# Latent attention: the five filler matmuls of a step in one group behind the transposes, instead of two in front and three behind

## What is computed

```python
q = (rmsnorm_2(c_q_raw, q_norm) @ w_uq)      # 8 heads x (64 + 32)
kv = (rmsnorm_2(c_kv_raw, kv_norm) @ w_ukv)  # 8 heads x (64 + 64)
s = (qn @ k_nope + qr @ k_rope) * scale      # per head and block of 128 queries
s = where(causal, s, -inf)
p = softmax(s)
o = p @ v
...
merged = sigmoid(gate_mla) * y_mla + sigmoid(gate_gdn) * y_gdn
```

## Time and profile before

| | |
|---|---|
| device time, three runs | 2192.75, 2192.87 and 2186.02 us (median 2192.75) |
| the profiled execution's own time | 2192.44 us |
| its span in the profile | 2190.4 us (2.0 us lie around it) |
| busy: TensorE matmul, VectorE, ScalarE, GpSimd | 94%, 38%, 34%, 36% of the span |
| the chain that ended last | 86% TensorE, 5% VectorE, 3% issue, 2% ScalarE, 2% GpSimd |
| mean granted clock of TensorE | 0.971 of full speed |
| the attention loop | from 1306.3 to 1425.2 us |

### The profile page before, as it was taken

One profiled execution on the slowest core, in us unless ns is written; L12 is line 12 of the kernel. 1 busy time (PEld: TensorE's weight loads), 2 busy tenths in 40 slices (PEclk: granted clock), 3 DMA queues, 4 the chain that ended last, 5 costly groups with the idle time before them and its releaser, 6 DMA issues.

```text
span 2190.4 us, 31427 instructions
## 1 busy us (share of the span) xinstructions
PE 2058.2 (94%) x13672; PEld 1765.2 (81%) x13672; DVE 831.7 (38%) x1270; ACT 737.1 (34%) x1089; POOL 781.8 (36%) x248
## 2 busy tenths in 40 slices
PE   7999999979988879999999989998998899999998
PEld 5898888858866669999999867797777678888886
DVE  3400675144357645220222141275466554211222
ACT  5332223236555534221223243332212333222222
POOL 4433223435422144434433421034313254434432
PEclk9999999989999989999999989998999999999999
DMA  4222221222210121323322420131013123223222
GB/s 167 96 96 92 73 68 58 96 67 82 93 57 20 39 77 58 97 73 102 97 75 90 102 82 29 46 95 60 21 55 112 43 93 96 92 84 114 92 65 75
DMA packets 172081, 171.48 MB, mean 78 GB/s; under 512 B 16924, under 2 KB 164760, under 8 KB 171944
## 3 DMA queue, kind: packets, MB, share of 16 engines
q1 hardware_dynamic: 170540, 167.25, 24.0%
q10 hardware_dynamic: 1404, 2.23, 0.3%
HBM read 163.17 MB, written 6.29 MB: 77 GB/s over the span
## 4 chain that ended last, share of the span: by engine, by line
PE 86%; DVE 5%; issue 3%; ACT 2%; POOL 2%; DMA 0%; ACTq 0%; DVEq 0%; SPq 0%; POOLq 0%
PE ps L2011 84%; PE ps L2013 2%; POOL w_lo L731 1%; POOL residual L754 1%; ACT w_hi L864 0%; DVE gdn_x L1883 0%; DVE sumsq L1319 0%; ACT diag L892 0%; DMA x_rows<-in_x 0%; DVE gdn_inv_t L1866 0%; POOL gdn_small L814 0%; POOL gdn_small L812 0%; DVE coef L1534 0%; DVE gdn_on L1956 0%; DVE mla_k L1688 0%
## 5 line engine op out<-in xcount | busy, mean ns | idle before, releaser
L731 POOL TENSOR_TENSOR w_lo<-w_raw,w_hi 128x2048 fp32r<-128x2048 f32 (+3 forms) x157 | 675.5, 4305 | 976.9 <-ACT w_hi L864 976.9
L2011 PE MATMUL ps<-u_hi,w_hi 128*128 128x512 f32 (+1 forms) x1904 | 596.3, 353 | 37.5 <-DVE sg L1522 12.3
L2011 PE MATMUL ps<-u_lo,w_hi 128*128 128x512 f32 (+1 forms) x1904 | 587.4, 348 | 0.0
L2011 PE MATMUL ps<-u_hi,w_lo 128*128 128x512 f32 (+1 forms) x1904 | 586.3, 348 | 0.0
L2011 PEld LDWEIGHTS ps<-u_hi,w_hi 128*128 128x128 f32 x1904 | 335.0, 192 | 85.1 <-issue 25.9
L2011 PEld LDWEIGHTS ps<-u_hi,w_lo 128*128 128x128 f32 x1904 | 334.1, 192 | 42.0 <-issue 0.7
L2011 PEld LDWEIGHTS ps<-u_lo,w_hi 128*128 128x128 f32 x1904 | 334.8, 192 | 38.8 <-issue 1.2
L864 ACT ACTIVATE w_hi<-w_raw 128x2048 fp32r<-128x2048 f32 (+3 forms) x157 | 279.4, 1783 | 176.4 <-PE ps L2011 167.1
L2011 PE MATMUL ps<-hidden_hi,w_hi 128*128 128x264 f32 (+1 forms) x528 | 141.1, 321 | 0.0
L2011 PE MATMUL ps<-hidden_lo,w_hi 128*128 128x264 f32 (+1 forms) x528 | 141.0, 322 | 0.0
L2011 PE MATMUL ps<-hidden_hi,w_lo 128*128 128x264 f32 (+1 forms) x528 | 140.8, 321 | 0.0
(11 more groups left out here) (368 smaller groups left out, 2921.7 us busy)
## 6 DMA issues: line engine op xcount, KB each, us to landing
w_raw<-in_w_in_a SPq DMA_DIRECT2D x23, 1024.0 KB, 5.2
w_raw<-in_ffn_w_gate SPq DMA_DIRECT2D x22, 1024.0 KB, 5.3
w_raw<-in_ffn_w_up SPq DMA_DIRECT2D x22, 1024.0 KB, 5.3
w_raw<-in_w_in SPq DMA_DIRECT2D x17, 1024.0 KB, 5.2
w_raw<-in_ffn_w_down SPq DMA_DIRECT2D x16, 768.0 KB, 4.4
w_raw<-in_ffn_w_down SPq DMA_DIRECT2D x16, 640.0 KB, 4.0
w_raw<-in_w_out_a SPq DMA_DIRECT2D x8, 1024.0 KB, 5.0
w_raw<-in_w_kv SPq DMA_DIRECT2D x8, 1024.0 KB, 5.3
```

Of the source, the lines that this page charges most:

```text
L731: pool.tensor_tensor(WL[:, u % RAWS, part], RAW[:, u % RAWS, part], WH[:, u % SPLITS, part].bitcast(F32), ALU.subtract).then_inc(lo_done, 1)
L2011: return nc.tensor.matmul(o, a, b, start=start, stop=stop, **kw)
```

## The change

```diff
         mla_fills, mla_filled, filled, rest = {}, {}, 0, False
         for step in range(HEADS * NT + MLA_LAG):
             mla_filled[step] = filled // FILL
-            for site, n in (("scored", 2), ("turned", 3)):
+            for site, n in (("scored", 0), ("turned", 5)):
                 n = 0 if rest or filled == FILL * MFILL_CHUNKS else min(n, FILL - filled % FILL)
                 mla_fills[step, site] = (filled, n)
                 filled += n
```

## The result

The changed kernel takes 2198.41 us (median of 22 runs, 2194.42 to 2207.85), the kernel before 2193.43 in 22 runs beside it. The ratio is 1.0031, 95% interval 1.0017 to 1.0045: slower by 0.3%. One of those 22 executions of the kernel before took 2580.61 us and isn't in the ratio, and the two medians alone lie 0.2% apart. Two later series of the unchanged pair gave 1.0018 (1.0000 to 1.0035) and 1.0008 (0.9989 to 1.0027). So the loss is clear in the first series and small in all three, 0.1 to 0.3%, against a forecast of -0.1%.

What follows compares the result with a forecast made beforehand. Only TensorE's time was taken to count, its waits and low clock in the attention loop. Terms -0.89 - 2.84 + 1.27 = -2.46 us took the median from 2192.75 to 2190.3 us; range 2183.5 to 2195.

Steps and rivals of the forecast that it cites:

- part 1: Attention loop, TensorE's stalls where filler chunks start: lost time falls from 6.65 to 5.76 us, gain 0.89 us.
- part 3: Attention loop, fillers covering the product's wait for `mla_norm`: lost cover grows from 0.73 to 2.00 us, loss 1.27 us.
- part 4: Attention loop: earlier transposes, `hi` and `lo` parts, stores and weight loads make nothing wait and cost nothing.
- part 2: Attention loop, low clock behind the stalls of steps 11 and 22: both low stretches go, gain 2.84 us.
- the price of 1.3 to 1.5: Attention loop: each low-clock stretch was taken to cost 1.3 to 1.5 us.
- rival 1: Low clock stays behind the stalls of steps 10 and 15: 2191.7 us with one stretch, 2193.1 with two; chance 0.23.
- rival 4: One to three low stretches elsewhere, behind the loop or in other stages, fall away: 2186.3 to 2188.9 us; chance 0.15.
- rival 2: Low clock also from step 31, without fillers, into the projection; three stretches with rival 1's two: 2194.5 us; chance 0.12.
- seven low stretches or a late `hi`: What a time above 2199.3 us would need, by the forecast; chance 0.02.

Runs made afterwards that it cites:

- after + 3.0: Changed kernel with 25 repeats of one projection matmul, 3.0 us, added behind the attention loop: ratio 1.0014 to the kernel before, loop 116.2 us.
- after + 1.5: Changed kernel with 7 matmuls of the mask's kind, 1.5 us, added directly in front of the attention loop: ratio 0.9984 to the kernel before, loop 116.2 us.
- the 40 matmuls: Changed kernel with 40 unread matmuls in TensorE's wait for `gdn_nk` at the delta net's start: ratio 0.9984 to the kernel before.
- before + 1.5: Kernel before with 7 matmuls of the mask's kind, 1.5 us, added in front of the attention loop: ratio 1.0026 to itself without them, delta net 194.8 us.

## Why the prediction was wrong

**Right: the stalls (part 1).** Idle times of 0.80, 1.14, 1.16, 0.66 and 0.68 us against 0.80, 1.14, 1.17, 0.65 and 0.80; in total 4.4 us in the view of waits against 4.6. Only step 25 was off, by 0.12.

**Right: the lost cover (part 3).** 1.82 us from mask to product in step 31 without fillers, idle 1.11 us against 1.1.

**Right: the free moves (part 4).** No wait of the transposes for `mla_pt`, none of the scores for `mla_exp` or a `hi` in the view of waits over the loop.

**Right as sums, wrong as a course: part 2.** The forecast loop is 118.9 - 2.46 = 116.4 us. Without low stretches the changed loop took 116.2 us in two profiles (after + 3.0, after + 1.5); with one it took 117.8, and the price of 1.3 to 1.5 says 117.7 to 117.9. But in the first two profiles and in the one with the 40 matmuls it took 119.3 or 119.4, with 6.8 us of low clock behind step 15, which cost 3.1 to 3.2 us and ate the whole gain of part 2. The step that failed is "after the change no stall of the loop is as long as these two ... I take both low stretches as gone". The length of the stall doesn't decide: the same 1.16 us of step 15 brought 6.8 us of low clock or none, and the stall of step 11 in the kernel before brought it or not (before + 1.5). This was rival 1, with 0.23, and it alone would have stayed inside the range. The Trainium skill, "TensorE: Matmul & The Clock Gate", Part 4, says that transposes don't count as TensorE being busy in the way matmuls do. The runs neither confirm nor refute that, and it doesn't decide here: the same transposes and the same 1.16 us stand in the loops with and without the low stretch.

**Wrong: the rest of the kernel as a constant.** The sum took all that follows the loop as shifted and otherwise unchanged; rival 4 let low stretches fall away there, rival 2 let one reach into the projection, and no rival had a loss in the delta net. The delta net lost 8.7 to 11.0 us in the first two profiles of the changed kernel, about four times the forecast change. With that, the range's top of 2195 failed, which was three low stretches at 1.3 to 1.5 us. The tail above 2199.3, "seven low stretches or a late `hi`", had 0.02; the median of 2198.41 stayed below it, but single executions went up to 2207.85. Low stretches don't come one by one at that price: one piece of 34.1 or 37.5 us in place of 10.2 cost 6.8 or 7.9 us, and a longer one near the delta net's end 1.9 or 3.2 more. The traces of before showed the place: a low stretch of 10.2 us lies over the delta net's start already, and TensorE waits there for 10.3 us. A range that took this in would have gone to about 2190.3 + 11 = 2201.

**Why it is slower on the average** is shown as far as the clock goes. The record has the mean granted clock of each execution. Call the span times (1 - clock) the lost clock. Over the 132 executions of the kernel before in the four later series the time grows by 0.64 us for each us of lost clock (correlation 0.95, scatter about it 1.2 us). The 45 executions of the changed kernel with nothing added have a mean of 2198.8 us and lie on that same line to 0.2 us, with a standard error of 0.2. So all of the average loss goes with more low clock, and none that can be seen is left for the order's own work. This is a correlation over executions.

What moves the low clock was shown for single courses. In 14 of the 18 profiles the loop, or the work added ahead of it, starts at the same distance from the low stretches ahead of it. There, with nothing added ahead of the loop, the kernel before meets two low stretches in the loop, and the changed one meets as much behind step 15 and, but for the 40 matmuls, the long one in the delta net as well. From the loop's start to the end of the span the kernel before takes 884.1 us in both profiles. The changed kernel takes 894.6, 893.2 and 885.3 us (span less the loop's start, 2186.9 - 1301.6 for the third), and moved by 1.5 us 882.5. How often each course comes in executions that aren't profiled isn't known, so the 0.1 to 0.3% can't be computed from the courses. Only the slow end can be counted: 7 of the changed kernel's 45 executions took over 2206 us, and of the 154 of the kernel before only the one of 2580.61. That work elsewhere can turn the sign is shown for one case, the 1.5 us in front of both. Why a given stall falls into a low stretch or not stays open.

## What to carry to other kernels

In a kernel whose trace shows scattered low stretches, as here, the stages of one program aren't independent: a change worth 1 or 2 us in one stage can cost or give some 10 us from there on by where it makes a later stage start. Before a change of this size is called good or bad, move the same code by a microsecond or two with idle work in both kernels; if that moves the time as much as the change does, as 1.5 us did here, the change hasn't been measured. Don't explain an average by one profile before looking where the profiled execution stands among all: here the first two stood at the slow end. And look at the stage in which the low clock lasts longest (here small matmuls behind a wait of 10.3 us). Filling that wait with 40 matmuls took the long piece out in the one profile of the changed kernel that had them; that it pays on the average isn't shown.

## What the hardware showed that was not expected

- The granted clock of one stage with the same instructions was 0.50 for 24 to 28 us on end in three profiles (first and second of the changed kernel, before + 1.5 us), 0.94 over 32 us in another (after + 1.5 us), and 1.00 with the 40 matmuls in the wait ahead of it. By the profile TensorE was busy for 27.5 of the 28 us, and the clock stayed low in them all the same.
- A stall of 1.16 us between the same neighbours was followed by 6.8 us at 1.2 GHz in three profiles of the changed kernel's loop and by none in four others (loops of 116.2, 116.2, 117.8 and 122.3 us; in the last the low clock came behind step 10 instead). The stall of 1.49 us in the kernel before was followed by low clock in seven of eight profiles of its loop, and not in the one with 1.5 us added.
- Where the low stretches ahead of the loop lie alike, the profiles repeat: the kernel before has the same low stretches in the same places to 0.1 us from the loop's start to the end (two profiles), and in the loop in four more that have work added only behind it, while the part ahead of the loop varies by 5.9 us. The changed kernel's third profile, with other low stretches ahead, took another course. Adding 1.5 us of work ahead of the loop made the kernel before 7.6 us slower from the loop's start to the end (884.1 to 891.7) and the changed kernel 12.1 us faster (894.6 to 882.5).
- The cost of a delay isn't its length: 0.5, 1.7 and 3.4 us of work behind the loop each made the kernel before about 3.3 us longer from the loop's start to the end (884.1 to 887.4 us).
